# One buffer for the high and low halves of a weight slot, word by word in turn

## The chip, the cores and the metric

The kernel runs on one core of a Trainium2 chip. The metric is the device time of one execution in microseconds (us). A core has TensorE (matrix products, results in PSUM), VectorE, ScalarE and GpSimd for elementwise work, and queues that start DMA transfers between HBM and SBUF, the memory on the core with 128 partitions. Semaphores order the engines' work.

## What is computed

The reference is two networks in a row on 256 tokens of 1024 channels, in float32. The first block is FFN, a mixer (gated delta rule over chunks of 64 beside dilated band attention), FFN, norm:

```python
x = x + 0.5 * swiglu(rms_norm(x, ffn1_norm[l]), ffn1_w_gate[l], ffn1_w_up[l], ffn1_w_down[l])
h = rms_norm(x, mix_norm[l])
proj = h @ w_in[l]
...
x = x + jnp.concatenate([o_a, o_b], axis=-1) @ w_out[l]
x = x + 0.5 * swiglu(rms_norm(x, ffn2_norm[l]), ffn2_w_gate[l], ffn2_w_up[l], ffn2_w_down[l])
```

The second block has two layers over the 256 tokens and, in the first of them, 256 context tokens as well: modulated FFNs (`swiglu_2`), a mixer of convolution, latent attention and Fourier branch, and a table of modulations `silu(c) @ w_ada`. Nearly all the work is products of activations with weights that are read once: `(jax.nn.silu(x @ w1) * (x @ w3)) @ w2` with 1024 and 2816 channels.

## The kernel before

Activations lie channels by tokens: 128 channels on the partitions, 256 tokens (first block, and second layer at the end) or 512 (tokens and context) along a row. A weight matrix is cut into tiles of 128x128, and a product takes such a tile as stationary operand and streams 256 or 512 columns of activations past it.

To keep float32 accuracy with the fast float32r format, each operand is cut in two: high = the value rounded to float32r, low = the rest. A product of tiles is then three matmuls, high x high, high x low, low x high, added up in PSUM (lines 1458 to 1460; 1473 to 1475 where two result tiles are filled in turn).

Weights come from HBM in the order of use as units of up to 1024 columns, eight tiles. A unit goes through three stages:

- SyncE's queue loads it into one of four slots of `w_raw` (lines 2498 and 2509), the refill as soon as the low half of the unit before in that slot is cut;
- ScalarE copies it into `w_hi` (line 1779), in one of three slots (`NH`), once TensorE is through with the unit three places earlier;
- VectorE subtracts `w_hi` from `w_raw` into `w_lo` (line 2075), and signals TensorE.

TensorE waits for `w_lo` of a unit before its first tile. `weight()` at line 1428 hands out the two stationary tiles as slices of 128 (sometimes 96 or 16) adjacent columns. In two places the weights are the streamed operand instead, 512 columns at a time, with activations as stationary operand: the values of the band attention (`v_mm`, lines 1526 to 1528) and of the latent attention (`vproj`, lines 1682 to 1684). The decay logits (`decay_mm`, lines 1492 to 1494) have stationary tiles of only 16 columns.

The order of all steps is written out ahead of time by `Plan`, one list that every engine walks through; `with_splits()` puts the splits into it, up to two units ahead (`AHEAD`). VectorE also sums the rows of the modulation table (lines 2068 and 2070), and does the FFN's products and splits (2115, 2117). The list does not depend on how long an instruction takes.

Products in full float32 (attention scores, transposes, delta rule; for instance lines 1701 and 1718) don't use the weight slots.

Of the kernel before, what the change touches and what calls it, by code (L numbers as in the profile page):

```python
# [10 lines left out]
F32R = mybir.dt.float32r  # L11
# [7 lines left out]
UC = 1024  # L19
NR, NH, AHEAD, LAG = 4, 3, 2, 2  # L20
# [1234 lines left out]
def build(nc, wstream, cols, consts, consts2, bias, xin, cvec, out):  # L1255
    with ExitStack() as stack:
        program(Plan(), nc, stack, wstream, cols, consts, consts2, bias, xin, cvec, out)


def program(plan, nc, stack, wstream, cols, consts, consts2, bias, xin, cvec, out):  # L1260
# [3 lines left out]
    def sb(name, shape, dt=F32, st=None):  # L1264
        return (st or stack).enter_context(nc.sbuf_tensor(name, shape, dt))
# [12 lines left out]
    MOD = MODT[:, 0:288].rearrange("p (l b v) -> p l b v", l=2, b=72)  # L1278
    banks = [stack.enter_context(nc.psum_tensor(f"B{i}", [128, 512], F32))[:] for i in range(8)]
    w_raw = sb("w_raw", [128, NR, UC])  # L1280
    w_hi, w_lo = sb("w_hi", [128, NH, UC], F32R), sb("w_lo", [128, NH, UC], F32R)
    CS, w_ada = sb("CS", [128, 2, 1024]), sb("w_ada", [128, 2, 1024])
    DER = sb("DER", [128, 2, 6, 8, 2])
    names = list(const_blocks())
# [1337 lines left out]
```

## Time and profile before

| | |
|---|---|
| runs | 2689.9, 2691.41, 2701.05 us; median 2691.41 |
| span of the profiled execution | 2690.7 us; the page gives no time of that execution beside its span |
| TensorE busy | 2603.1 us (97%), 15924 matmuls |
| TensorE weight loads busy | 2305.4 us (86%) |
| VectorE busy | 1693.8 us (63%) |
| ScalarE busy | 1083.8 us (40%) |
| DMA | 380.98 MB, 142 GB/s on average |
| granted TensorE clock, mean | 0.988 |

The span is the time from the first instruction to the last. Busy time is the union of an engine's instruction records; matmul records overlap, so the time from one start to the next is what a matmul costs in a dense stretch. The granted clock is a share of 2.4 GHz.

### The profile page before, as it was taken

The numbers are of one execution on the slowest core, as the hardware profiler recorded it, in microseconds if no ns is written. First come the engines' busy times: TensorE is split into PE (matmuls) and PEld (weight loads), VectorE is DVE, ScalarE is ACT, GpSimd is POOL, SyncE is SP. The second block draws the span as 40 slices with busy tenths as digits, with TensorE's granted clock in tenths as the row PEclk, the third lists the DMA queues.
The fourth block names the chain that finished last, engine by engine and source line by source line (L and its number), as shares of the span: only waits on it lengthen the run. The fifth ranks groups of instructions, "written<-read, shape, count | busy, mean of one in ns | idle before, by whom it ended". The sixth has DMA issues, their size and how long they took to land.

```text
span 2690.7 us, 38911 instructions
## 1 busy us (share of the span) xinstructions
PE 2603.1 (97%) x15924; PEld 2305.4 (86%) x15924; DVE 1693.8 (63%) x2685; ACT 1083.8 (40%) x1686; POOL 64.2 (2%) x60
## 2 busy tenths in 40 slices
PE   7999899999999999999999999999999999998998
PEld 7998789899888888778888888889888888888998
DVE  6767555777777655656644777755555446786664
ACT  5546643555322224344253422223322234555553
POOL 0001021000000000000000000000000000000000
PEclk9999899999999999999999999999999999999999
DMA  7764201576455443111223455543444433244454
GB/s 262 235 230 175 86 9 48 191 236 208 150 178 189 169 150 103 50 47 63 94 91 98 135 190 178 180 162 111 141 133 137 133 113 111 78 131 157 169 193 147
DMA packets 110113, 380.98 MB, mean 142 GB/s; under 512 B 12016, under 2 KB 17392, under 8 KB 109552
## 3 DMA queue, kind: packets, MB, share of 16 engines
q1 hardware_dynamic: 108928, 373.32, 42.2%
q10 hardware_dynamic: 1008, 5.18, 0.5%
q8 instruction: 126, 2.06, 0.3%
q14 instruction: 51, 0.42, 0.1%
HBM read 377.40 MB, written 1.05 MB: 141 GB/s over the span
## 4 chain that ended last, share of the span: by engine, by line
PE 88%; DVE 5%; ACT 4%; issue 2%; DMA 0%; SPq 0%; ACTq 0%; DVEq 0%
PE B L1458 25%; PE B L1460 25%; PE B L1459 25%; ACT w_hi L1779 2%; DVE w_lo L2075 2%; PE B L1718 1%; PE B L1701 1%; PE B L1473 1%; PE B L1611 1%; PE B L1474 1%; PE B L1625 1%; PE B L1475 1%; PE B L1618 1%; PE B L1708 1%; DVE AC L2324 1%
## 5 line engine op out<-in xcount | busy, mean ns | idle before, releaser
L1458 PE MATMUL B<-U,w_hi 128*128 128x256 f32 (+1 forms) x2896 | 962.1, 332 | 6.3 <-DVE w_lo L2075 6.2
L1459 PE MATMUL B<-U,w_hi 128*128 128x256 f32 (+1 forms) x2896 | 952.8, 329 | 0.0
L1460 PE MATMUL B<-U,w_lo 128*128 128x256 f32 (+1 forms) x2896 | 952.6, 329 | 0.0
L2075 DVE TENSOR_TENSOR w_lo<-w_raw,w_hi 128x1024 fp32r<-128x1024 f32 (+3 forms) x587 | 685.5, 1180 | 410.1 <-ACT w_hi L1779 409.0
L1779 ACT ACTIVATE w_hi<-w_raw 128x1024 fp32r<-128x1024 f32 (+3 forms) x587 | 591.0, 1012 | 500.1 <-PE B L1460 477.8
L1458 PEld LDWEIGHTS B<-U,w_hi 128*128 128x128 f32 x2896 | 547.1, 189 | 62.9 <-issue 8.2
L1459 PEld LDWEIGHTS B<-U,w_hi 128*128 128x128 f32 x2896 | 546.7, 189 | 53.3 <-issue 2.2
L1460 PEld LDWEIGHTS B<-U,w_lo 128*128 128x128 f32 x2896 | 546.7, 189 | 51.4
L1458 PE MATMUL B<-HHf,w_hi 128*128 128x256 f32 (+1 forms) x1122 | 364.3, 325 | 1.8 <-DVE w_lo L2075 1.8
L1460 PE MATMUL B<-HHf,w_lo 128*128 128x256 f32 (+1 forms) x1122 | 363.5, 324 | 0.0
L1459 PE MATMUL B<-HLf,w_hi 128*128 128x256 f32 (+1 forms) x1122 | 363.5, 324 | 0.0
L1841 ACT ACTIVATE HHf<-TMP 128x256 fp32r<-128x256 f32 (+1 forms) x132 | 69.4, 525 | 413.7 <-DVE TMP L2115 413.7
L1458 PEld LDWEIGHTS B<-HHf,w_hi 128*128 128x128 f32 x1122 | 211.3, 188 | 20.5 <-DVE w_lo L2075 2.4
L1459 PEld LDWEIGHTS B<-HLf,w_hi 128*128 128x128 f32 x1122 | 211.3, 188 | 18.1
L1460 PEld LDWEIGHTS B<-HHf,w_lo 128*128 128x128 f32 x1122 | 211.3, 188 | 17.9
L2115 DVE TENSOR_TENSOR TMP<-TMP,B 128x256 f32<-128x256 f32 (+1 forms) x132 | 73.0, 553 | 178.3 <-PE B L1460 175.3
L2070 DVE CUSTOM_DVE_ANT_0 w_ada<-w_ada,CS 128x1024 f32<-128x1024 f32 x144 | 175.9, 1222 | 0.0
L2068 DVE CUSTOM_DVE_ANT_0 TMP<-w_ada,CS 128x1024 f32<-128x1024 f32 x144 | 175.6, 1220 | 0.0
L2117 DVE TENSOR_TENSOR HLf<-TMP,HHf 128x256 fp32r<-128x256 f32 (+1 forms) x132 | 73.9, 560 | 78.1 <-ACT HHf L1841 78.1
L2324 DVE SCALAR_TENSOR_TENSOR AC<-VC,PC,AC 128x512 f32<-128x512 f32 (+1 forms) x180 | 103.6, 627 | 0.1
L1784 ACT ACTIVATE TMP<-X 128x256 f32<-128x256 f32 (+1 forms) x76 | 35.4, 477 | 162.4 <-DVE X L2128 144.9
L2128 DVE SCALAR_TENSOR_TENSOR X<-B,DER,X 128x256 f32<-128x256 f32 x80 | 36.2, 480 | 63.9 <-PE B L1460 63.9
(352 smaller groups left out, 2620.2 us busy)
## 6 DMA issues: line engine op xcount, KB each, us to landing
w_raw<-in_w SPq DMA_DIRECT2D x504, 512.0 KB, 4.3
w_ada<-in_w SPq DMA_DIRECT2D x144, 512.0 KB, 3.4
w_raw<-in_w SPq DMA_DIRECT2D x58, 384.0 KB, 3.1
w_raw<-in_w SPq DMA_DIRECT2D x16, 240.0 KB, 2.5
X<-in_x SPq DMA_DIRECT2D x2, 1024.0 KB, 9.6
w_raw<-in_w SPq DMA_DIRECT2D x8, 256.0 KB, 2.6
BW<-in_bias ACTq DMA_DIRECT2D x1, 1536.0 KB, 10.3
K<-in_consts ACTq DMA_DIRECT2D x2, 640.0 KB, 4.9
```

What stands on the lines that cost most here:

```text
L1458: pe.matmul(o, hi, xh, start=i == 0 and s.start, stop=False)
L1459: pe.matmul(o, hi, xl, start=False, stop=False)
L1460: e = pe.matmul(o, lo, xh, start=False, stop=i == last and s.stop)
L1779: act.activation(w_hi[:, plan.slot[u], 0:n], w_raw[:, plan.ring[u], 0:n], ACT.Copy).then_inc(*up("w_hi", u))
L1841: act.activation(HI[p][:, j, :], TM(s.t, s.n), ACT.Copy).then_inc(*up("hh", s.key))
L2068: dve.tensor_tensor_reduce(tmp[:, 5:7, :].rearrange("p a b -> p (a b)"), raw, CS[:, 0, :], 1.0, 0.0, ALU.mult, ALU.add, MOD[:, l, b, 0:1]) ...
L2070: dve.tensor_tensor_reduce(raw, raw, CS[:, 1, :], 1.0, 0.0, ALU.mult, ALU.add, MOD[:, l, b, 1:2]).then_inc(*up("ada", s.key, ("unit", u)))
L2075: dve.tensor_tensor(w_lo[:, plan.slot[u], 0:n], w_raw[:, plan.ring[u], 0:n], w_hi[:, plan.slot[u], 0:n].bitcast(F32), ALU.subtract).then_i ...
L2115: dve.tensor_tensor(h, h, PS(s.b2, s.n), ALU.mult).then_inc(*up("hm", s.key))
L2117: dve.tensor_tensor(LO[p][:, j, :], h, HI[p][:, j, :].bitcast(F32), ALU.subtract).then_inc(*up("hl", s.key))
L2128: dve.scalar_tensor_tensor(out=X[:, m, c], in0=PS(s.b)[:, c], scalar=DER[:, l, 3 + i, m, h:h + 1], in1=X[:, m, c], op0=ALU.mult, op1=ALU.a ...
L2324: dve.scalar_tensor_tensor(out=AC[:, c], in0=VC[:, c, :, i:i + 256], scalar=col(f"w_dw{l}", 31 * c + i), in1=AC[:, c], op0=ALU.mult, op1=A ...
```

## The change

The two buffers become one with a fourth dimension of two words; `w_hi` and `w_lo` are its even and odd words. Everything else reads them through the same names.

```diff
     w_raw = sb("w_raw", [128, NR, UC])
-    w_hi, w_lo = sb("w_hi", [128, NH, UC], F32R), sb("w_lo", [128, NH, UC], F32R)
+    w_cut = sb("w_cut", [128, NH, UC, 2], F32R)
+    w_hi, w_lo = w_cut[:, :, :, 0], w_cut[:, :, :, 1]
     CS, w_ada = sb("CS", [128, 2, 1024]), sb("w_ada", [128, 2, 1024])
```

The accesses that have a step of two words (8 bytes) from now on: the write at line 1779, the read and the write at line 2075, the stationary operands at lines 1458 to 1460, 1473 to 1475 and 1492 to 1494, and the streamed operands at 1526 to 1528 and 1682 to 1684. The buffer has the same size as the two together and stands in their place.

## Rows read from the trace of the kernel before

**Rows 1.** The page: span, and the chain that ended last by engine.
```profile
span 2690.7 us, 38911 instructions
...
PE 88%; DVE 5%; ACT 4%; issue 2%; DMA 0%; SPq 0%; ACTq 0%; DVEq 0%
```

**Rows 2.** Groups by form: busy us, mean ns of one, idle before and its releasers.
```profile
L2075 DVE TENSOR_TENSOR w_lo<-w_raw,w_hi 128x1024 fp32r<-128x1024 f32 x504 | 615.4, 1232 | 376.3 <-ACT w_hi L1779 375.6
...
L1779 ACT ACTIVATE w_hi<-w_raw 128x1024 fp32r<-128x1024 f32 x504 | 529.2, 1054 | 490.1 <-PE B L1460 467.9 <-PE B L1475 16.1 <-PE B L1528 4.4
L1458 PE MATMUL B<-U,w_hi 128*128 128x512 f32 x1288 | 504.4, 392 | 0.0
...
L1458 PE MATMUL B<-U,w_hi 128*128 128x256 f32 x1592 | 450.6, 283 | 6.3 <-DVE w_lo L2075 6.2
...
L1458 PE MATMUL B<-HHf,w_hi 128*128 128x256 f32 x660 | 184.3, 279 | 1.8 <-DVE w_lo L2075 1.8
...
L1458 PE MATMUL B<-HHf,w_hi 128*128 128x512 f32 x462 | 180.0, 390 | 0.0
...
L1473 PE MATMUL B<-U,w_hi 128*128 128x256 f32 x208 | 64.2, 309 | 10.6 <-DVE U L2090 8.0 <-DVE U L2107 2.6
```

**Rows 3.** Stretches: us, busy us (count) of PE, PEld, DVE, ACT, POOL, clock, DMA.
```profile
203.00:207.00 4.00, 4.00 (x20) 4.00 (x20) 3.85 (x11) 2.09 (x5) 0.00 (x0) 0.50 0.11 40
500.00:650.00 150.00, 149.97 (x1323) 149.77 (x1322) 114.80 (x162) 74.78 (x110) 0.00 (x0) 1.00 0.71 234
700.00:1000.00 300.00, 300.00 (x1325) 248.65 (x1324) 204.22 (x301) 83.08 (x103) 0.00 (x0) 1.00 0.52 174
2500.00:2690.00 190.00, 182.48 (x1586) 181.86 (x1584) 108.72 (x142) 88.57 (x126) 0.00 (x0) 0.98 0.50 170
214.00:228.00 14.00, 14.00 (x73) 11.93 (x72) 11.01 (x12) 6.90 (x10) 10.54 (x7) 1.00 0.73 265
```

**Rows 4.** Timeline of TensorE, 256 columns: start us, duration us, instruction.
```profile
99.75 0.28 PE L1459 MATMUL B<-U,w_hi 128*128 128x256 f32 x1
...
101.91 0.28 PE L1460 MATMUL B<-U,w_lo 128*128 128x256 f32 x1
```

**Rows 5.** Timeline of TensorE, 512 columns.
```profile
999.62 0.39 PE L1460 MATMUL B<-HHf,w_lo 128*128 128x512 f32 x1
...
1004.83 0.39 PE L1459 MATMUL B<-HLf,w_hi 128*128 128x512 f32 x1
```

**Rows 6.** Timeline of TensorE, 256 columns of another streamed tile.
```profile
1469.73 0.28 PE L1459 MATMUL B<-Y0L,w_hi 128*128 128x256 f32 x1
...
1470.81 0.28 PE L1459 MATMUL B<-Y0L,w_hi 128*128 128x256 f32 x1
```

**Rows 7.** Timeline of TensorE, stationary tiles of 16 columns.
```profile
308.73 0.28 PE L1492 MATMUL B<-U,w_hi 128*16 128x256 f32 x1
...
309.87 0.28 PE L1493 MATMUL B<-U,w_lo 128*16 128x256 f32 x1
```

**Rows 8.** Timeline of TensorE, 256 columns, in the first stretch of rows 3.
```profile
203.19 0.41 PE L1474 MATMUL B<-U,w_hi 128*128 128x256 f32 x1
...
205.96 0.41 PE L1475 MATMUL B<-U,w_lo 128*128 128x256 f32 x1
```

**Rows 9.** Timeline of TensorE, full float32, merged runs (x counts them).
```profile
2301.38 5.32 PE L1701 MATMUL B<-QK 96*128 96x512 f32 x12
...
2320.17 3.68 PE L1718 MATMUL B<-V,w_ada 128*128 128x64 f32 x32
```

**Rows 10.** Line 1528 alone: ns min/median/max, first and last start us, form.
```profile
L1528 PE MATMUL B<-w_hi,U x16: 393/395/397, 216.5 to 226.8; 128*128 128x512 f32 x16
```

**Rows 11.** Line 1682 alone.
```profile
L1682 PE MATMUL B<-w_hi,CK0H x8: 389/390/482, 1100.3 to 1105.2; 128*128 128x512 f32 x8
```

**Rows 12.** Waits: who waited for whom, us in total, times, longest.
```profile
PE B L1458 <- DVE w_lo L2075: 14.4, 18, 2.4
```

## The prediction

> **What bounds the kernel now.** I read the page first: the span, then the chain of work that ended last. 88% of the span is TensorE's own work, and DMA has no share [rows 1]. So the question is how fast TensorE takes one tile after another, and what might stop it. The groups of instructions give the counts [rows 2]. The products that read a weight slot as stationary operand come three to a tile of 128x128: 1592 + 660 + 208 = 2460 tiles stream 256 columns, 1288 + 462 = 1750 tiles stream 512. That is 7380 and 5250 matmuls. Their records overlap, so a duration there is not a cost; the cost is the distance between starts, from the timeline. At 256 columns 19 steps take 101.91 - 99.75 us, 113.7 ns each [rows 4]; at 512 columns 23 steps take 5.21 us, 226.5 ns each [rows 5]. 7380 x 0.1137 + 5250 x 0.2265 = 839 + 1189 = 2028 us, three quarters of the span. The stretches say the same: TensorE is busy 149.97 of 150 us and 300 of 300 us, at a granted clock of 1.00 (2.4 GHz) [rows 3].
>
> VectorE is the second engine: 114.8 of 150 us (77%) in a stretch of 256 columns, 204.2 of 300 us (68%) in one of 512 [rows 3]. ScalarE is at 50% and 28%. TensorE waits for a finished low half 18 times, 14.4 us in all [rows 12], so the splitting is hidden nearly everywhere.
>
> **The change, part by part.** No instruction, wait, transfer or byte is added or taken away. The one buffer has the size of the two and their place, so no other tensor moves. What changes is the step, from one word to two, in four kinds of access.
>
> (1) Loading the stationary tile, once for every matmul, 12,630 times in the two big groups. The trace has no such load with a step, so I bound it. The plain rows: where only 64 columns are streamed, a load of 128 columns is the longer part, and 32 of them take 3.68 us, (3.68 - 0.28) / 31 = 110 ns each, with 0.28 us for the last record as in rows 4 [rows 9]. That is only 4 ns less than the distance at 256 columns. At 256 columns a load has therefore no reserve; at 512 it has 117 ns. Lower end: the load stays at 110 ns, nothing changes. Upper end: each word costs twice, 220 ns; then 256 columns go at 220 instead of 114 ns, 7380 x 0.106 = +782 us, and 512 columns (226.5 ns) still cover it. I take the lower end, because of the nearest row for what a read of the array can do: the streamed operand passes 512 words in 226.5 ns [rows 5], 2.26 words per ns, while a load passes 128 words in 110 ns, 1.16 per ns. A load that skips every second word covers 2.33 words of address per ns, what the other read does already within 3%. Sum: 0.
>
> (2) Streaming weights with the step: L1526 to L1528 (16 each) and L1682 to L1684 (8 each in either layer), 48 + 48 = 96 matmuls of 512 columns [rows 10, 11]. Here the step would mean 4.5 words of address per ns, and no row shows that speed. Lower end 0. Upper end half speed: the full-precision matmuls stream 512 columns in 5.32 / 12 = 443 ns at most [rows 9], so 96 x (443 - 227) = +20.7 us. TensorE is busy 14.00 of 14 us around the first 48 [rows 3], so half of it is surely on the path; behind it, waits of the mixer may swallow some. I keep 0 to 21 us and take 0 for the forecast; with the two ends about equally near, the upper end is a rival of its own.
>
> (3) Writing the high half on ScalarE (504 of 1054 ns) and (4) reading it and writing the low half on VectorE (504 of 1232 ns) [rows 2]. A full-size unit holds 8 tiles, which TensorE uses up in 24 x 0.1137 = 2.73 us at 256 columns and 5.44 us at 512. Lower end 0. Upper end, every word costs twice: VectorE gets 1.232 us more per unit, 45% of a stretch of 256 columns, 77 + 45 = 122%, over the bound; priced among the rivals. At 512 it gets 68 + 23 = 91% and stays hidden. I take 0: these engines pass one word in 1.03 and 1.20 ns, overhead included, half the rate or less at which TensorE reads the same memory, so a step of two words asks less of it than TensorE's contiguous stream does. If the cover of 23% of VectorE were gone, each further 0.1 us per split would cost 4% of the stretches of 256 columns, as they are bound then.
>
> Two rules of the Trainium skill bear on this, and they disagree. "Advanced Engine Details and Errata", section "Memory Cachelines", has lines of 16 bytes that want at least two hits in a row for full speed. A step of two words gives exactly two; by that rule (1), (3) and (4) cost nothing. "Vector Engine (DVE) Microarchitecture Reference", section 5.2, speaks against the change: a port keeps its rate only for runs of at least two adjacent words, and a destination that hops with every element costs 1.71 ns per column in place of 1.054. A step of two words is not in its table. By it a split takes some 1.90 in place of 1.23 us, an estimate from that page, and the time would be about 2700 us; its worst entry (2.5 ns per column) comes out above the doubling below. No row of this trace shows a step on a long operand, so neither is borne out yet.
>
> (5) What the two reads of TensorE do to each other. The distance at 256 columns is 113.7 ns in one place and (1470.81 - 1469.73) / 9 = 120 ns in another [rows 4, 6], same instruction, other address of the streamed tile. So addresses matter by 6 ns a matmul. The step changes how the load runs through the addresses. Yet a load of only 16 columns leaves (309.87 - 308.73) / 10 = 114 ns [rows 7], so most of what stands above 256 / 2.4 = 107 ns is not made by the load. At a granted clock of 0.50 (1.2 GHz) 256 columns take (205.96 - 203.19) / 13 = 213 ns, with nothing above 256 / 1.2 [rows 3, 8]: at half speed there is no collision. Worst: all 256-column matmuls at 120 and all 512 ones 6.5 ns later: 7380 x 0.0063 + 5250 x 0.0065 = +81 us. Best: nothing above the pure stream, 7380 x 0.007 + 5250 x 0.0132 = -121 us. I take 0, since rows 7 say that the load has little part in it.
>
> Sum: 2690.7 + 0 = 2690.7 us of span. The page gives no time beside the span; the median of the three runs (2689.9 to 2701.05) is 0.7 us above it. Forecast 2691.4 us.
>
> **The rivals.** A, the streamed weights at half speed, (2): 2691.4 + 20.7, less 4 us that I allow for mixer waits: 2708 us. For it: no row shows the speed it would need. Against: only 96 matmuls. Chance 0.16.
> B, the load is dearer or collides: +81 us gives 2772 us; if the load doubles, 2691.4 + 782 = 3473 us. It decides as soon as a load takes over 114 ns. For it: 4 ns of reserve and the 6 ns by address. Against: the speed of the other read, rows 7. Chance 0.08 each. This is the one that ends clearly on the other side.
> C, the splits cost twice: VectorE bound at 122% in the dense half of the 839 us (+22%, 92 us), at 57 + 45 = 102% in the rest, as 2500 to 2690 us shows [rows 3] (+2%, 8 us): 2791 us. It decides from a split of 1.23 / 0.45 x 0.23 + 1.23 = 1.86 us on. Chance 0.12.
> D, collisions go away, since load and stream now run through the addresses at one speed: between 2690 us, where the 120 ns become 114 in the few places, and 2570 us. Halfway, 2631 us, is its time. For it: rows 8 and the 120 ns. Against: rows 7. Chance 0.20.
> That the change does nothing to the access can't be: the step is in the operands.
>
> **How the numbers follow.** No change 0.36, A 0.16, B 0.16, C 0.12, D 0.20. A measurement of this kernel tells 0.5% (13.5 us) from no change. Faster by more: most of D and an edge of the forecast, 0.17. Slower by more: B, C, most of A, 0.42. Within: 0.41. The range is 2630 to 2795 us; it leaves out the doubled load (0.08), the lower part of D and what lies above C, 0.2 together. The forecast alone is 2683 to 2700 us.
>
> **What would show it.** Step (1): loads of L1458 stay at 188 to 189 ns, starts 113 to 114 and 227 ns apart; wrong if 256 columns go at 120 ns or more. (2): starts of L1526 and L1682 stay near 228 ns; wrong near 440. (3), (4): L1779 stays at 1054 and L2075 at 1232 ns; wrong if either grows and TensorE's wait for w_lo leaves 14 us behind. (5): the share of 120 ns distances. A change of the starts in either direction at an unchanged load would make the forecast wrong in its core.

## The result, and the profile after

The change costs 4%: median 2801.73 us (2796.29 to 2804.54, four runs) against 2690.65 us (2688.2 to 2701.05, four runs), ratio of the means 1.0404 with a 95% interval of 1.0381 to 1.0427. The profiled execution took 2798.95 us, its span is 2797.1 us, 106.4 us more than before [rows 1]. The forecast was no change; 2802 us lies above its range as well.

The page, the span and the chain that ended last:

```profile
span 2797.1 us, 38911 instructions
...
PE 89%; DVE 5%; ACT 4%; issue 2%; DMA 0%; SPq 0%; ACTq 0%; DVEq 0%
```

The number of instructions is that of [rows 1], and so is the make-up of the chain within a point (PE 89% for 88%). TensorE is the bound as before, and each of its matmuls takes longer. The groups of instructions by form (busy us, mean ns of one, idle before and its releasers), to be held against [rows 2]:

```profile
L2076 DVE TENSOR_TENSOR w_cut<-w_raw,w_cut 128x1024 fp32r<-128x1024 f32 x504 | 613.7, 1228 | 443.6 <-ACT w_cut L1780 442.8
L1780 ACT ACTIVATE w_cut<-w_raw 128x1024 fp32r<-128x1024 f32 x504 | 575.8, 1147 | 524.4 <-PE B L1461 494.1 <-PE B L1476 16.6 <-PE B L1529 12.2
L1459 PEld LDWEIGHTS B<-U,w_cut 128*128 128x128 f32 x2880 | 565.1, 196 | 61.0 <-issue 7.4 <-DVE w_cut L2076 4.1 <-ACT SMALL L1946 0.2
...
L1459 PE MATMUL B<-U,w_cut 128*128 128x512 f32 x1288 | 515.2, 400 | 0.0
...
L1459 PE MATMUL B<-U,w_cut 128*128 128x256 f32 x1592 | 456.9, 287 | 7.5 <-DVE w_cut L2076 7.2
```

VectorE's split is where it was (1228 for 1232 ns). TensorE's load records are a little longer (196 for 189 ns). ScalarE's copy is 9% longer (1147 for 1054 ns), and TensorE waits no longer for the halves, as two more views say. The stretches (us; busy us and count of PE, PEld, DVE, ACT, POOL; clock; DMA) have no idle TensorE, with VectorE at 68% and 67%:

```profile
50.00:200.00 150.00, 150.00 (x1253) 150.00 (x1252) 102.39 (x138) 73.53 (x95) 0.00 (x0) 1.00 0.66 220
700.00:1000.00 300.00, 300.00 (x1332) 252.22 (x1331) 200.31 (x299) 91.75 (x115) 0.00 (x0) 1.00 0.48 163
```

The waits (total us, times, longest) for a low half are as good as those of [rows 12], 14.6 for 14.4 us:

```profile
PE B L1459 <- DVE w_cut L2076: 14.6, 16, 2.4
```

So the time is in the distance between matmuls. Timeline of TensorE after, in five places (start us, duration us): 256 columns, 512 columns, streamed weights, 256 columns at half clock, and stationary tiles of 16 columns:

```profile
100.00 0.28 PE L1461 MATMUL B<-U,w_cut 128*128 128x256 f32 x1
...
102.40 0.28 PE L1460 MATMUL B<-U,w_cut 128*128 128x256 f32 x1
...
1009.75 0.40 PE L1460 MATMUL B<-HLf,w_cut 128*128 128x512 f32 x1
...
1014.70 0.40 PE L1460 MATMUL B<-HLf,w_cut 128*128 128x512 f32 x1
...
228.34 0.65 PE L1527 MATMUL B<-w_cut,U 128*128 128x512 f32 x1
...
230.61 0.65 PE L1529 MATMUL B<-w_cut,U 128*128 128x512 f32 x1
...
213.16 0.41 PE L1475 MATMUL B<-U,w_cut 128*128 128x256 f32 x1
...
215.93 0.41 PE L1476 MATMUL B<-U,w_cut 128*128 128x256 f32 x1
...
331.53 0.28 PE L1493 MATMUL B<-U,w_cut 128*16 128x256 f32 x1
...
333.98 0.28 PE L1493 MATMUL B<-U,w_cut 128*16 128x256 f32 x1
```

- 256 columns: 20 steps in 2.40 us, 120 ns; before 113.7 [rows 4], 113.3 over the whole stretch from 500 to 600 us.
- 512 columns: 21 steps in 4.95 us, 235.6 ns; before 226.5 [rows 5].
- Streamed weights: 5 steps in 2.27 us, 454 ns; before 226 to 232 in the same place.
- Half clock (granted clock 0.50, 1.2 GHz, from 213 to 216 us): 13 steps in 2.77 us, 213 ns, exactly as before [rows 8]. There the step is free.
- Tiles of 16 columns: 21 steps in 2.45 us, 117 ns; before 114 [rows 7].

All such distances added up (each below 600 ns, between two matmuls in a row that both read a weight slot) give 989.3 for 949.7 us at 256 columns and 1411.8 for 1345.5 us at 512 columns: 39.6 + 66.3 = 105.9 us of the 106.4 us. Of the 66.3 us, 20.9 us are the streamed weights, which start 453.7 ns apart in place of 231.7.

### The profile page after: what moved, and what is told of

The parts are those of the page before. It is cut to its first block, busy times and chain, and to the rows that moved or that the text cites. A ratio compares the mean times of both kernels' runs of the same rounds, so it can differ in the third digit from the quotient of the medians.

```text
span 2797.1 us, 38911 instructions
## 1 busy us (share of the span) xinstructions
PE 2710.0 (97%) x15924; PEld 2394.0 (86%) x15924; DVE 1692.5 (61%) x2685; ACT 1133.5 (41%) x1686; POOL 62.2 (2%) x60
## 4 chain that ended last, share of the span: by engine, by line
PE 89%; DVE 5%; ACT 4%; issue 2%; DMA 0%; SPq 0%; ACTq 0%; DVEq 0%
PE B L1459 25%; PE B L1461 25%; PE B L1460 25%; ACT w_cut L1780 2%; DVE w_cut L2076 1%; PE B L1719 1%; PE B L1702 1%; PE B L1474 1%; PE B L1475 1%; PE B L1612 1%; PE B L1476 1%; PE B L1626 1%; PE B L1709 1%; PE B L1619 1%; DVE AC L2325 1%
## 5 line engine op out<-in xcount | busy, mean ns | idle before, releaser
L1459 PE MATMUL B<-U,w_cut 128*128 128x256 f32 (+1 forms) x2896 | 979.2, 338 | 7.5 <-DVE w_cut L2076 7.2
L2076 DVE TENSOR_TENSOR w_cut<-w_raw,w_cut 128x1024 fp32r<-128x1024 f32 (+3 forms) x587 | 684.7, 1177 | 480.5 <-ACT w_cut L1780 479.1
L1461 PE MATMUL B<-U,w_cut 128*128 128x256 f32 (+1 forms) x2896 | 968.4, 334 | 0.0
L1460 PE MATMUL B<-U,w_cut 128*128 128x256 f32 (+1 forms) x2896 | 966.5, 334 | 0.0
L1780 ACT ACTIVATE w_cut<-w_raw 128x1024 fp32r<-128x1024 f32 (+3 forms) x587 | 642.4, 1101 | 534.0 <-PE B L1461 503.7
L1459 PEld LDWEIGHTS B<-U,w_cut 128*128 128x128 f32 x2896 | 567.7, 196 | 62.3 <-issue 7.9
L1461 PEld LDWEIGHTS B<-U,w_cut 128*128 128x128 f32 x2896 | 565.7, 195 | 54.5
L1460 PEld LDWEIGHTS B<-U,w_cut 128*128 128x128 f32 x2896 | 565.9, 195 | 51.2 <-issue 2.2
L1459 PE MATMUL B<-HHf,w_cut 128*128 128x256 f32 (+1 forms) x1122 | 371.2, 331 | 1.3 <-DVE w_cut L2076 1.3
L1461 PE MATMUL B<-HHf,w_cut 128*128 128x256 f32 (+1 forms) x1122 | 370.1, 330 | 0.0
L1460 PE MATMUL B<-HLf,w_cut 128*128 128x256 f32 (+1 forms) x1122 | 369.1, 329 | 0.0
L1459 PEld LDWEIGHTS B<-HHf,w_cut 128*128 128x128 f32 x1122 | 219.6, 196 | 19.1 <-DVE w_cut L2076 1.7
L1461 PEld LDWEIGHTS B<-HHf,w_cut 128*128 128x128 f32 x1122 | 218.7, 195 | 19.6
L1460 PEld LDWEIGHTS B<-HLf,w_cut 128*128 128x128 f32 x1122 | 218.8, 195 | 17.4
L2129 DVE SCALAR_TENSOR_TENSOR X<-B,DER,X 128x256 f32<-128x256 f32 x80 | 36.2, 479 | 66.3 <-PE B L1461 66.3
```

The lines of the kernel that those rows point to most:

```text
L1459: pe.matmul(o, hi, xh, start=i == 0 and s.start, stop=False)
L1460: pe.matmul(o, hi, xl, start=False, stop=False)
L1461: e = pe.matmul(o, lo, xh, start=False, stop=i == last and s.stop)
L1780: act.activation(w_hi[:, plan.slot[u], 0:n], w_raw[:, plan.ring[u], 0:n], ACT.Copy).then_inc(*up("w_hi", u))
L2076: dve.tensor_tensor(w_lo[:, plan.slot[u], 0:n], w_raw[:, plan.ring[u], 0:n], w_hi[:, plan.slot[u], 0:n].bitcast(F32), ALU.subtract).then_i ...
L2129: dve.scalar_tensor_tensor(out=X[:, m, c], in0=PS(s.b)[:, c], scalar=DER[:, l, 3 + i, m, h:h + 1], in1=X[:, m, c], op0=ALU.mult, op1=ALU.a ...
```

## The experiments

In the table are all kernels that ran, with what the timelines show: distances between starts in dense stretches. The ratio of the means, with its 95% interval, is to executions of the kernel before taken beside each kernel, whose medians are 2690.65 us (after), 2695.32 us (e1, e2, e3, p16), 2700.21 us (p32, p0_48, w48, step4), 2696.57 us (the three q) and, for e3_again, one execution of 2690.48 us. So the medians of two groups compare only to some 10 us. The diffs show the deciding lines alone.

| kernel | median us | ratio | 256 columns, ns | 512 columns, ns |
|---|---|---|---|---|
| before | 2690.65 | 1 | 113.3, in places 117.8 or 120 | 226.7 |
| after | 2801.73 | 1.0404 [1.0381, 1.0427] | 120 | 233 to 238 |
| e1_streamed_plain | 2774.56 | 1.0293 [1.0267, 1.0320] | 120 | as after |
| e2_read_step_only | 2773.84 | 1.0285 [1.0264, 1.0306] | 120 | 233 to 238 |
| e3_write_step_only | 2705.68 | 1.0029 [1.0011, 1.0047] | 113.3 or 117.8 | 226.7 |
| e3_again | 2717.56 (one run) | none | 117.8, in places 113.3 | 226.7 |
| step4_read_only | 3602.25 (one run) | none | 233 to 238 | 235 |
| p16_after | 2789.04 | 1.0342 [1.0318, 1.0366] | 120 | 233.3 |
| p32_after | 2785.00 | 1.0318 [1.0288, 1.0348] | 120 to 121 | 231.4 |
| p0_48_after | 2768.12 | 1.0256 [1.0226, 1.0286] | 120 | 230 |
| w48_before | 2734.82 | 1.0132 [1.0103, 1.0162] | 120, in places 113.3 to 117.8 | 226 to 232 |
| q48_8_before | 2739.51 | 1.0143 [1.0110, 1.0175] | 113.3 or 117.8 | 233.3 |
| q56_4_before | 2745.04 | 1.0172 [1.0150, 1.0194] | 118.3 | 230 to 234 |
| q40_60_before | 2731.59 | 1.0119 [1.0096, 1.0141] | 117 to 119 | 226.7 or 236.7 |

### Which access costs: streamed, stationary or written

**e1_streamed_plain** is the changed kernel, except that the eight units that are streamed (`v_mm` and `vproj`) keep their halves side by side, without a step.

```diff
+    streamed = {wt[0] for s in plan.steps if s.kind in ("v_mm", "vproj") for wt in s.wts}
+    def part_of(u, w, a, b):
+        if u in streamed:
+            return w_cut[:, plan.slot[u], w * UC + a:w * UC + b]
+        return turns[:, plan.slot[u], a:b, w]
```

> The changed kernel, but the eight units whose weights are streamed (lines 1526 to 1528 and 1682 to 1684 of before) keep their halves one after the other inside the same buffer. In the profile after, these 96 matmuls start 453 ns apart in place of 227 to 232. Theory L (three costs: the stepped load beside the streamed read, the stepped stream, nothing else): 96 x 0.224 = 21.5 us less, about 2780 us, starts at 227 to 232 ns again, all other distances as after. Rival, mixer waits had swallowed part: 5 to 15 us less.

Measured: 27 us less than after by the medians, 26.5 us by the spans (2770.6 us). Timeline of TensorE, streamed weights:

```profile
228.04 0.40 PE L1535 MATMUL B<-w_cut,U 128*128 128x512 f32 x1
...
229.65 0.39 PE L1533 MATMUL B<-w_cut,U 128*128 128x512 f32 x1
```

7 steps in 1.61 us, 230 ns in place of 454. The streamed operand with a step of two words goes at half speed, and all of it is on the path: 96 x 0.222 = 21.3 us from the distances. The 5 us beyond that, of the measured 26.5, were not followed up; the four spans of the kernel after (2794.5 to 2802.7) lie 8 us apart.

**e2_read_step_only** goes back to the kernel before and its two buffers. Only the order of columns inside a unit is changed: two stationary tiles stand column by column in turn, so that TensorE reads either with a step of two words, while ScalarE and VectorE write without one. Streamed units stay as they were, and so do the tiles of 16 columns.

```diff
-        return w_hi[:, plan.slot[u], c:c + m], w_lo[:, plan.slot[u], c:c + m]
+        a, step = woven(plan.units[u][2]).get(c, (c, 1))
+        cols = slice(a, a + step * (m - 1) + 1, step)
+        return w_hi[:, plan.slot[u], cols], w_lo[:, plan.slot[u], cols]
```

> The kernel before, high and low halves in two buffers, all writes contiguous; only the stationary tiles are read with a step of two words: two tiles of a unit stand column by column in turn (the weights arrive in that order). Streamed weights are contiguous. Theory L (the step of the load itself is what costs): distances 120 to 122 ns at 256 columns and 233 to 238 at 512, as after, 2690.7 + 80 = 2770 us, ScalarE's split back at 1054 ns. Rival I (the halves being neighbours, one line of memory for both, costs): 2691 us and 113/227 ns. Rival W (the stepped writes disturb TensorE's reads): 2691 us.

Timeline of TensorE, 256 and 512 columns:

```profile
99.80 0.28 PE L1479 MATMUL B<-U,w_hi 128*128 128x256 f32 x1
...
102.32 0.28 PE L1479 MATMUL B<-U,w_hi 128*128 128x256 f32 x1
...
1009.69 0.40 PE L1479 MATMUL B<-HHf,w_hi 128*128 128x512 f32 x1
...
1014.87 0.40 PE L1480 MATMUL B<-HLf,w_hi 128*128 128x512 f32 x1
```

120 ns (21 steps) and 235.5 ns (22 steps), as after. The tiles of 16 columns, which have no step here, are back at 113.9 ns on average; after they have it and stand at 116.7. ScalarE's copy, from the groups, is back at 1055 ns:

```profile
L1800 ACT ACTIVATE w_hi<-w_raw 128x1024 fp32r<-128x1024 f32 x504 | 529.8, 1055 | 537.2 <-PE B L1481 515.3 <-PE B L1496 15.8 <-PE B L1549 4.4
```

Span 2771.0 us, e1's within 0.4 us. The step of the stationary read alone gives the whole remainder; that high and low words are neighbours, and that they are written with a step, adds nothing that these two kernels show.

**e3_write_step_only** is the counterpart: TensorE reads as before, and the two splits write with the step (the columns of a unit are laid out in HBM to match).

```diff
-                act.activation(w_hi[:, plan.slot[u], 0:n], w_raw[:, plan.ring[u], 0:n], ACT.Copy)
+                act.activation(odd_even(w_hi[:, plan.slot[u], 0:n]), halves_of(w_raw[:, plan.ring[u], 0:n]), ACT.Copy)
```

> The kernel before, but ScalarE and VectorE write the halves (and VectorE reads the high one) with a step of two words, even columns first, then the odd ones; the weights arrive in an order that puts every column in its old place, and TensorE reads contiguously as before. Theory L: 2691 us, 113/227 ns, ScalarE's split 1147 ns as after and hidden. Rival W (stepped writes disturb TensorE's reads): distances of 120 and 233 and about 2770 us.

The groups:

```profile
L1785 ACT ACTIVATE w_hi<-w_raw 128x1024 fp32r<-128x1024 f32 x504 | 571.3, 1138 | 477.6 <-PE B L1466 452.9 <-PE B L1481 17.4 <-PE B L1534 4.1
...
L2081 DVE TENSOR_TENSOR w_lo<-w_raw,w_hi 128x1024 fp32r<-128x1024 f32 x504 | 615.1, 1232 | 396.1 <-ACT w_hi L1785 395.3
```

ScalarE takes 1138 ns, VectorE 1232: the step costs the one 8 to 9% and the other nothing. But the time rose by 0.29% (ten runs, 2696 to 2713 us), which neither theory had. The profiled span is 13.7 us longer than that of the kernel before, and 11 us of it are distances at 256 columns; 512 columns didn't change. The timeline of TensorE in two places shows how:

```profile
49.73 0.28 PE L1466 MATMUL B<-U,w_lo 128*128 128x256 f32 x1
...
52.11 0.28 PE L1466 MATMUL B<-U,w_lo 128*128 128x256 f32 x1
...
549.77 0.28 PE L1465 MATMUL B<-U,w_hi 128*128 128x256 f32 x1
...
552.24 0.28 PE L1465 MATMUL B<-U,w_hi 128*128 128x256 f32 x1
```

113.3 ns in one stretch, 117.6 ns in another, same instructions and same buffers. Either the stepped writes reach TensorE in some stretches, or there are two rhythms that a dense stretch can fall into by how it starts. **e3_again** is the same kernel once more.

> The write-step-only kernel once more, for its profile alone. In its first profile 256 columns ran at 113.3 ns from 0 to 200 us and at 117.8 from 475 to 650, with the same stepped writes beside both. Theory R (at a distance of 48 words the matmuls have two rhythms, 113.3 and 117.8 ns, and keep the one that a stretch happened to start in): some stretch has the other rhythm this time. Rival W (the writes do it): the same stretches have the same rhythm again.

Its timeline, at the place where the first profile had 113.3 ns:

```profile
49.80 0.28 PE L1464 MATMUL B<-U,w_hi 128*128 128x256 f32 x1
...
52.28 0.28 PE L1464 MATMUL B<-U,w_hi 128*128 128x256 f32 x1
```

118 ns, with the same program at the same place. It isn't so all through: from 470 us on the same execution has 113.3 ns (42 steps in 4.76 us).

```profile
470.36 0.28 PE L1464 MATMUL B<-U,w_hi 128*128 128x256 f32 x1
...
475.12 0.28 PE L1464 MATMUL B<-U,w_hi 128*128 128x256 f32 x1
```

The kernel before, which writes nothing with a step, has the slower value too, at a granted clock of 1.00: 117.6 ns (42 steps) beside the 113.7 of [rows 4].

```profile
2244.16 0.28 PE L1458 MATMUL B<-U,w_hi 128*128 128x256 f32 x1
...
2249.10 0.28 PE L1458 MATMUL B<-U,w_hi 128*128 128x256 f32 x1
```

So either value comes with the stepped writes and without them. There are two rhythms. In these three traces a dense stretch keeps the one that it has as long as it streams from the same buffer, and the next stretch may have the other: the first profile of e3 has 113.3 ns from 462 to 471 us, then TensorE pauses and runs at half clock for 4 us, and from 484 us on it has 117.8. What picks it was not found, and whether the stepped writes make the slower one more frequent, which would explain the 0.29%, isn't shown.

### Why the stationary read costs: its rate, or its address against the stream's

**step4_read_only** is e2 with four tiles in turn, a step of four words (`WOVEN = 4`).

> As the read-step-only kernel, but four tiles of a unit stand column by column in turn, so that a load has a step of four words. If the load is bound by how many lines of 16 bytes it touches (theory L with lines: 32 at step one, 64 at step two, 128 here): a load takes 210 to 230 ns in place of 110, 256 columns go at about 220 ns, 512 columns at 240 or more: 3450 to 3600 us. If it is bound by words and only collisions cost (rival C): the same as step two, 120 and 233 to 238 ns, about 2774 us.

Timeline, and the group of the loads:

```profile
99.75 0.40 PE L1481 MATMUL B<-U,w_lo 128*128 128x256 f32 x1
...
102.81 0.40 PE L1479 MATMUL B<-U,w_hi 128*128 128x256 f32 x1
```

```profile
L1480 PEld LDWEIGHTS B<-U,w_hi 128*128 128x128 f32 x2880 | 927.6, 322 | 0.8
```

235 ns (13 steps) at 256 columns, the load being the bound now, and 235 ns at 512 columns as well, where such a load is also longer than the plain stream's 226.7 ns. One limit fits all reads of TensorE seen here within 4%, some 2.2 words of address per ns: a plain stream 512 / 226.7 = 2.26; a stream with a step of two 1024 / 454 = 2.26; a load with a step of four 512 / 235 = 2.18. A load with a step of two would need 256 / 2.26 = 113 ns by the first two or 256 / 2.18 = 117.5 ns by the last, both estimates; none was measured by itself. So of the 6.7 ns at 256 columns up to 4 may be its rate. At 512 columns it can't be: the load is done within 120 ns, as the distance at 256 columns shows, has over 100 ns to spare, and costs 9 ns all the same. Nor can it be at the tiles of 16 columns, whose load is an eighth as long and costs 3 ns. What remains there is the meeting of the two reads.

The addresses test that. In the kernel before, streamed tiles of 256 columns begin at word 48 of a block of 64, and those of 512 at word 0. Three kernels move them under the changed one, `P` being the two places (256, 512); the cut leaves out the same edit for the low halves and the hidden tiles:

```diff
-    HI = {f"U{i}": U[:, 48 - 48 * i:4144 - 48 * i].rearrange("p (k t) -> p k t", k=8) for i in range(2)}
+    P = (16, 16)   # or (32, 32), (0, 48)
+    HI = {f"U{i}": U[:, P[i]:P[i] + 4096].rearrange("p (k t) -> p k t", k=8) for i in range(2)}
```

> The changed kernel, but the streamed tiles start 16 words past a multiple of 64 for both 256 and 512 columns (after: 48 and 0). Theory L (with a step of two words every place of the streamed tile meets the load): no change within 0.3%, 120 to 122 and 233 to 238 ns. Rival P (the step only moves the good place, and another place gets 113/227 ns back): at this place 113 or 227 ns in one of the two lengths, 40 to 50 us less for that length.

> The changed kernel with the streamed tiles 32 words past a multiple of 64, for both lengths. Theory L (a load with a step of two meets the streamed read wherever that starts): 120 and 233 to 234 ns, 2789 us like at 16 words. Rival P: this is the good place, 113 or 227 ns again for one length, 40 to 50 us less.

> The changed kernel with the places of the streamed tiles exchanged: 256 columns start at a multiple of 64 words, 512 columns 48 words past it (after: the other way round). Theory L: 120 and 233 to 234 ns; the 238 ns of the first of three matmuls of 512 columns, seen only at place 0, gone: 2785 to 2792 us. Rival P: 113 or 227 ns again for one length.

512 columns with places (16, 16), and the same stretch with (0, 48):

```profile
900.01 0.40 PE L1461 MATMUL B<-U,w_cut 128*128 128x512 f32 x1
...
904.92 0.40 PE L1461 MATMUL B<-U,w_cut 128*128 128x512 f32 x1
```

```profile
900.00 0.39 PE L1460 MATMUL B<-U,w_cut 128*128 128x512 f32 x1
...
904.83 0.39 PE L1460 MATMUL B<-U,w_cut 128*128 128x512 f32 x1
```

233.8 and 230 ns (21 steps each). The mean over all stationary tiles at 512 columns falls with the place: 234.9 at word 0, 233.3 at 16, 231.4 at 32, 230.2 at 48. That gives back about a third of the loss (2768 us for (0, 48)), while 256 columns stay at 120 to 121 ns in every place. The load has the same step in all four, so at 512 columns the cost depends on where the two reads stand; at 256 it doesn't, and these runs don't part rate from meeting there.

**w48_before** leaves the step out and moves the weight slots to word 48 of a block of 64, in the kernel before. `U` ends 16 words earlier, so that the slots, and the buffers between it and them, begin 16 words earlier; 16 words behind the slots (not in the cut) keep the rest in place:

```diff
-    U = sb("U", [128, 2 * 4096 + 64], F32R)
+    U = sb("U", [128, 2 * 4096 + 48], F32R)
```

> The kernel before, step of one word, streamed tiles at their old places (48 and 0), but the weight slots start 48 words past a multiple of 64, so that the distance of load and stream in addresses is 0 at 256 columns (as where 120 ns were seen) and 16 at 512. If load and stream collide by their relative address (theory L): 256 columns go from 113 to about 120 ns, some 45 us more; 512 columns have not been seen at this distance, 227 or 233 ns. If the place of the streamed tile alone decides (rival S): 113 and 227 ns, 2691 us.

256 and 512 columns:

```profile
99.72 0.28 PE L1460 MATMUL B<-U,w_hi 128*128 128x256 f32 x1
...
102.36 0.28 PE L1461 MATMUL B<-U,w_lo 128*128 128x256 f32 x1
...
899.93 0.39 PE L1459 MATMUL B<-U,w_hi 128*128 128x512 f32 x1
...
904.96 0.39 PE L1460 MATMUL B<-U,w_hi 128*128 128x512 f32 x1
```

120 ns (22 steps) without any step in an operand, and 228.6 ns (22 steps). Here the streamed tiles of 256 columns stand where they stood; of what TensorE reads in these products only the loaded ones moved. The places where the kernel before had 120 ns (256 columns streamed from a buffer laid out for 512) went to 113.3 to 117.8 ns at the same time. The very instruction of [rows 6], 120 ns there:

```profile
1491.08 0.28 PE L1460 MATMUL B<-Y0L,w_hi 128*128 128x256 f32 x1
...
1497.20 0.28 PE L1460 MATMUL B<-Y0L,w_hi 128*128 128x256 f32 x1
```

113.3 ns (54 steps). So it is not a bad address of either read that costs 6 to 7 ns, it is a bad place of load and stream against each other. The Trainium skill says otherwise ("TensorE: Matmul & The Clock Gate", section "Step-by-step: what each phase is for"): the two SBUF reads of TensorE have ports of their own, and loading the next tile takes no read bandwidth from the running matmul. Here one shift of the loaded tiles takes matmuls from 113.3 to 120 ns, and the measurement decides.

Three more kernels sought a better pair of places under the kernel before, all with the edit of `P`.

> The kernel before (step one, plain halves), with the 512-column tiles 8 words past a multiple of 64 in place of 0; 256-column tiles stay at 48. The 256-column matmuls on 512-column tiles (about 1100, 120 ns at distance 0) had 114 to 118 ns at a distance of 16 words, where 512 columns took 226 to 231. Theory L (only the relative address counts): at 8 words 512 columns stay at 227 and these 1100 fall to 114: 7 us less, 2684 us. Rival: 512 columns rise to 229 as at 16 words, 5250 x 0.0015 = 8 us more, and it comes out even.

> The kernel before with 256-column tiles at 56 words and 512-column tiles at 4. Theory L: if the good distances form one stretch, 56 (8 words short of meeting) is as good as 48, 113 ns, and 4 words still give 227 ns: 2691 us or up to 7 us less. Rival: the good places are single points, and one of the lengths goes to 117 to 120 or 233: 30 to 45 us more.

> The kernel before with 256-column tiles at 40 words and 512-column tiles at 60, 4 words short of meeting. Theory L gives no number for 60, between 233 ns at 48 and 227 at 0: if the edge lies before 60, 227 ns and 2691 us; else 233 ns, 5250 x 0.0066 = 35 us more. 256 columns at 40: 113 ns as at 48, or up to 120 and 45 us more.

512 columns with the place 8:

```profile
899.86 0.40 PE L1461 MATMUL B<-U,w_lo 128*128 128x512 f32 x1
...
905.00 0.40 PE L1459 MATMUL B<-U,w_hi 128*128 128x512 f32 x1
```

233.6 ns (22 steps), where I had expected 227. All three are slower than before, by 1.2 to 1.7%. In q48_8_before the 256-column tiles didn't move, and yet they ran at 117.8 ns in the early stretches and at 113.3 in the last: the two rhythms again. Here a stretch changes over without a pause: 117.8 ns up to 649.3 us, three distances of 123 to 124 ns, and 113.3 ns from then on, from the same buffers. So a rhythm can be left within a stretch too. In q40_60_before 512 columns have two rhythms as well, with the same buffer and a granted clock of 1.00: 236.7 ns (18 steps) and 226.7 ns (21 steps).

```profile
870.39 0.40 PE L1459 MATMUL B<-U,w_hi 128*128 128x512 f32 x1
...
874.65 0.40 PE L1459 MATMUL B<-U,w_hi 128*128 128x512 f32 x1
...
1599.68 0.39 PE L1459 MATMUL B<-U,w_hi 128*128 128x512 f32 x1
...
1604.44 0.39 PE L1459 MATMUL B<-U,w_hi 128*128 128x512 f32 x1
```

So one profile doesn't always tell what a place costs. No place tried here beat those of the kernel before, and no rule that I had for a good place survived.

## Why the prediction was wrong

**(1), the load by itself: no doubling, but not shown to be free.** The sign set for this step, wrong if 256 columns go at 120 ns or more, came true, and the load records went from 189 to 196 ns. The doubling (3473 us) did not come; step4_read_only has it at four words. A load with a step of two takes 120 ns at most, since 256 columns go at that distance; how much of the 6.7 ns is its own is open, up to 4 ns by step4's rate, an estimate. The ground given for taking 0, that a load with the step covers address no faster than the stream does, holds within 4%, and with 4 ns of reserve 4% matter. The 110 ns of the plain load came from products in full float32, not from the float32r loads that the change touches. The Trainium skill ("Advanced Engine Details and Errata", section "Memory Cachelines": 16-byte lines, two hits a line for full speed) agrees with the load within these few ns, at most 120 ns at two words and 235 ns at four; it doesn't with the streamed operand, which has two hits a line and took 454 ns.

**(2), streamed weights: the failed term of second size.** Taken as 0 with an upper end of +20.7 us; the upper end came in full, 21.3 us by distances and 26.5 us by e1. The text had noted that no row shows the speed that this access would need. The stream's speed in [rows 5] was the only row for what a read can do, and it held as a ceiling. The 4 us allowed for waits of the mixer didn't appear either.

**(3), (4), the splits: right in effect.** VectorE kept 1232 ns, ScalarE went from 1054 to 1147 ns, and its 93 ns are hidden, TensorE's wait for low halves staying at 14.6 us. The rule of the Trainium skill that runs of at least two adjacent words are wanted ("Vector Engine (DVE) Microarchitecture Reference", section 5.2; 1.90 us for a split by its price) is not borne out for a step of two words: 1.228 us.

**(5), the meeting of the two reads: the step that failed.** It stood as "I take 0, since rows 7 say that the load has little part in it". Its upper end was 7380 x 0.0063 + 5250 x 0.0065 = +81 us; measured were +39.6 us at 256 columns and 66.3 - 20.9 = +45.4 us at 512, together 85 us. e2 shows that the step of the load alone makes it, 80.3 us of span. The end had the path and the 120 ns; that its size is so near is in part luck, since 256 columns lost 5.1 ns on average instead of 6.3 (some were at 117.8 or 120 ns before) and 512 columns 8.0 instead of 6.5. At 512 columns and at tiles of 16 the loss is the meeting of the reads; at 256 a part of it may be the load's rate, (1). The forecast picked the other end by a wrong reading of a row. The 114 ns with tiles of 16 columns [rows 7] were read as a matmul with hardly any load, so that the load couldn't matter. But 114 ns is what a well-placed full load gives as well. The row shows the price at a good place; it has nothing of a bad one. [Rows 6] had that, 120 ns for the same instruction, and was put down to the address of the streamed tile alone. w48_before shows that it is the place of one read against the other, and the three kernels with other places show that with a step of two words in the load 256 columns stand at 120 to 121 ns wherever the stream begins. What was already at 120 ns before stayed at 120.

**Rivals.** A and B's first case happened together, 21 + 85 us, and nothing in the prediction joined them: 2691 + 21 + 81 = 2793 us, with chances of 0.16 and 0.08 given separately. C's 2791 us is the nearest of the single rivals by luck: its mechanism did not occur. D, that collisions would go, is refuted: no distance at 2.4 GHz fell.

**Open.** How long a load with a step of two takes by itself, why two reads at these places get in each other's way, what sets which of 113.3 and 117.8 ns a stretch has, and why 512 columns improve steadily from word 0 to 48 under the changed kernel, while under the one before no place tried beat word 0.

## What to carry to other kernels

Where TensorE's matmuls stand back to back, read the distance between starts for each pair of streamed and stationary buffer: two values for one instruction mean that a change of layout may move all the matmuls from one to the other. Look for both values within one pair first, since a program can show two without any change. A step of two words doubled the time of the streamed operand here; in the stationary one it cost 3 to 6% of the distance, and no place tried gave 113 or 227 ns back. And when two small costs have no row, add up their upper ends once before taking both as nothing.

## What the runs showed of the hardware

- Streamed and stationary reads of TensorE interact: 113.3 or 120 ns at 256 columns, 226.7 or up to 236 ns at 512, by relative place alone (w48_before, 256 columns) or by a step in the load (e2_read_step_only). At 1.2 GHz (213 ns for 256 columns, before and after) there is no such cost.
- A streamed operand with a step of two words took 454 ns for 512 columns in place of 227 to 232; a load with a step of four words 235 ns (step4_read_only).
- A dense stretch at 256 columns can run at 113.3 or at 117.8 ns with the same program, and mostly keeps its value; the kernel before shows both in one execution, and q48_8_before one change over within a stretch, after three distances of 123 to 124 ns. The two profiled executions of e3 have spans of 2704.4 and 2715.8 us, and 7.5 of the 11.4 us are such distances. At 512 columns q40_60_before shows 226.7 and 236.7 ns.
- An operand with a step of two words costs ScalarE's write 8 to 9% (1138 and 1147 for 1054 ns) and VectorE's read and write nothing (1228 and 1232 for 1232 ns).
